# The second block's projections and its last product in three rounded passes each, with x kept in memory in between

## The reference, cut to what matters

```python
h = rms_norm_2(x, norm_g) * (1 + scale[:, None, :]) + shift[:, None, :]
proj = h @ w_in
q, kcr, vcr, ksl, vsl, kwn, vwn, z_a, g_br, u, z_s = jnp.split(proj, offs, axis=-1)
...
attn = nsa_attention(q, kc, vc, k_slc, kv_heads(vsl), k_win, kv_heads(vwn), gates)
attn = attn * jax.nn.silu(z_a)
y = s5_mixer(u, ssm_a_re, ssm_a_im, ssm_log_dt, ssm_b_re, ssm_b_im, ssm_c_re, ssm_c_im, ssm_d)
y = jax.nn.gelu(y)
y = y * jax.nn.sigmoid(y @ glu_w.astype(jnp.float32) + glu_b.astype(jnp.float32))
ssm = y.astype(x.dtype) * jax.nn.silu(z_s)
mix = jnp.concatenate([attn, ssm], axis=-1) @ w_out
return x + gate[:, None, :] * mix
```

## Time and profile before

| | us |
|---|---|
| median of 3 runs | 1591.18 (1590.16 to 1595.38) |
| the profiled execution | 1588.68 |
| its span (first to last instruction) | 1586.8 |
| TensorE busy | 1432.6 (90%) |
| VectorE busy | 950.3 (60%) |
| ScalarE busy | 511.9 (32%) |
| GpSimd busy | 52.7 (3%) |
| second block from its first product to the GLU | 1144.4 to 1348.4 |
| attention pairs | 1397.7 to 1528.2 |
| last product, from its first halves to its last matmul | 1519.35 to 1579.1 |

### The profile page before, as it was taken

The page is one execution under the profiler, slowest core; times in us unless marked ns, Lnnn a source line. Parts: engine busy times, 40 slices in busy tenths (PEclk is TensorE's granted clock), DMA queues, the critical chain, the costliest instruction groups (busy, mean ns, idle before and its releaser), DMA issues.

```text
span 1586.8 us, 18674 instructions
## 1 busy us (share of the span) xinstructions
PE 1432.6 (90%) x7046; PEld 1092.9 (69%) x7046; DVE 950.3 (60%) x1601; ACT 511.9 (32%) x824; POOL 52.7 (3%) x43
## 2 busy tenths in 40 slices
PE   5998888896989877999899999999798999988998
PEld 4758788785567655787688888888567954566653
DVE  6259767676166768774545545533493748868730
ACT  5346332331322554233323423423313221223310
POOL 0000000000000450000000000000000002000000
PEclk9999999997989979999899999999898999989999
DMA  5212111121222120353134443222421122520001
GB/s 223 75 53 81 67 41 54 61 90 49 84 107 80 47 74 27 136 209 107 53 136 156 186 159 143 73 77 106 133 82 37 58 76 80 186 80 1 1 1 53
DMA packets 39881, 140.49 MB, mean 89 GB/s; under 512 B 13041, under 2 KB 17521, under 8 KB 27249
## 3 DMA queue, kind: packets, MB, share of 16 engines
q1 hardware_dynamic: 34608, 130.53, 23.4%
q10 hardware_dynamic: 5184, 8.78, 1.5%
HBM read 128.42 MB, written 8.39 MB: 86 GB/s over the span
## 4 chain that ended last, share of the span: by engine, by line
PE 54%; DVE 4%; ACT 1%; issue 1%; ACTq 0%; DVEq 0%
PE turn L700 22%; PE score L685 7%; PE score L700 5%; PE sum L685 4%; PE turn L685 3%; PE sum L700 2%; PE sum L1263 2%; PE sum L1145 1%; PE score L1145 1%; PE score L1237 1%; PE turn L1249 1%; PE turn L822 1%; DVE stat L2541 1%; PE turn L1118 1%; DVE probs L1774 0%
## 5 line engine op out<-in xcount | busy, mean ns | idle before, releaser
L1816 DVE TENSOR_TENSOR ring_r<-ring,heads_r 128x1024 fp32r<-128x1024 f32 (+3 forms) x153 | 176.3, 1153 | 222.6 <-ACT heads_r L1359 187.2
L1359 ACT ACTIVATE heads_r<-ring 128x1024 fp32r<-128x1024 f32 (+3 forms) x153 | 153.4, 1002 | 241.0 <-DMA ring<-wstream 129.2
L700 PE MATMUL score<-h_sb_r,heads_r 128*128 128x512 f32 x376 | 151.6, 403 | 0.0
L700 PE MATMUL turn<-tiles_r,heads_r 128*128 128x512 f32 x336 | 132.2, 393 | 0.0
L700 PE MATMUL turn<-h_sb_r,heads_r 128*128 128x512 f32 x304 | 119.7, 394 | 8.1 <-DVE ring_r L1816 8.1
L700 PE MATMUL turn<-wide_r,heads_r 128*128 128x512 f32 x312 | 121.9, 391 | 0.0
L700 PE MATMUL turn<-wide_r,ring_r 128*128 128x512 f32 x312 | 121.6, 390 | 0.0
L700 PE MATMUL score<-x_sb_r,heads_r 128*128 128x512 f32 x256 | 110.1, 430 | 8.9 <-DVE ring_r L1816 6.5
L700 PE MATMUL score<-x_sb_r,ring_r 128*128 128x512 f32 x256 | 103.8, 405 | 0.0
L700 PEld LDWEIGHTS score<-h_sb_r,heads_r 128*128 128x128 f32 x376 | 73.9, 197 | 13.9 <-issue 0.2
L700 PEld LDWEIGHTS turn<-tiles_r,heads_r 128*128 128x128 f32 x336 | 64.1, 191 | 13.3
(11 more groups left out here) (399 smaller groups left out, 2952.5 us busy)
## 6 DMA issues: line engine op xcount, KB each, us to landing
ring<-wstream SPq DMA_DIRECT2D x95, 1024.0 KB, 4.9
ring<-wstream SPq DMA_DIRECT2D x16, 704.0 KB, 4.4
ring<-gated SPq DMA_DIRECT2D x6, 1024.0 KB, 6.9
gated<-tiles ACTq DMA_DIRECT2D x15, 256.0 KB, 2.0
gated<-probs ACTq DMA_DIRECT2D x9, 256.0 KB, 2.0
x_sb<-xT SPq DMA_DIRECT2D x4, 512.0 KB, 5.7
x_sb<-xT ACTq DMA_DIRECT2D x1, 2048.0 KB, 8.3
outT<-x_sb SPq DMA_DIRECT2D x1, 2048.0 KB, 6.3
```

The costliest lines, as they stand in the source:

```text
L700: return pe.matmul(out, a, w, **k) if moving else pe.matmul(out, w, a, **k)
L1359: step(act.activation(head_piece(p), chunk(name)[:, c:c + cols], ACT.Identity), f"head {p}")
L1816: step(dve.tensor_tensor(out, a, b, op), name)
```

## The change

- The chunks of `w_in` and `w_out` of the second block get pieces: 23 for `w_in` (22 of 1024 columns, one of 192), 8 for `w_out`. All products with them go through `triple`. In the first pair of products TensorE follows the splits k by k (`split_pair`).
- The rounded activations of the norm need two buffers. The head goes where x lies (`X_HEAD` in `x_sb`), the remainder into `h_sb`. So ScalarE stores each of the eight tiles of x to memory (`gated`) as soon as it is complete and loads all back (2 MB) behind the last product of `w_in`.
- The heads of the 23 pieces get six places of their own (`PLACES2`: an unused constant, the mask `chosen`, four pairs of tiles), since `heads` holds state-space data there. `heads_through` says how many ScalarE makes after each drain: one to four pieces ahead.
- The remainders of all 31 pieces, the scaling of x (16 operations instead of VectorE's 8), the splits of the four state-space tiles and of three attention tiles are GpSimd's. VectorE splits the norm (8 operations more) and the last attention tile.
- Order: 14 products instead of 9 after the first ones stand ahead of the matrices (2 whole, 12 row), so 3 row products more than before; `SIDE` is 5, 5, 4, 4, and 18 are left, so no product is left for behind the last y.
- `w_out`: four banks instead of two take first halves: two in the place of the 33rd pair, one ahead of the last turn, one behind it; then four second halves and four whole products.

```diff
-    proj2 = [(f"proj2_{i}", len(c) * tile) for i, c in enumerate(by_twos(PROJ2))]
-    out += proj2[:2] + [(f"rows2_{n}", KD * width(parts)) for n, parts in ROWS2] + proj2[2:]
+    proj2 = [(f"proj2_{i}", [tile] * len(c)) for i, c in enumerate(by_twos(PROJ2))]
+    out += proj2[:2] + [(f"rows2_{n}", [KD * 24] if n == "g" else [tile, tile]) for n, _ in ROWS2] + proj2[2:]
...
-    out += [(f"wout2_{i}", 2 * tile) for i in range(4)]
+    out += [(f"wout2_{i}", [tile] * 2) for i in range(4)]
...
-    SIDE = [5, 5, 5, 4]
+    SIDE = [5, 5, 4, 4]
...
+    WIDE_HEAD = H_REST
+    WIDE_REST = [TL_REST[:, 6 + k if k < 4 else k - 2, :] for k in range(KD)]
+    WIDE_BANKS = [score[:, z * T:(z + 1) * T] for z in range(4)]
...
+    FIRST2, WOUT2 = piece_of["proj2_0"][0][0], piece_of["wout2_0"][0][0]
+    PLACES2 = [cst_r[:, coff["level"][0]:coff["level"][0] + PIECE], chosen_r[:, :]] + \
+              [tiles_r[:, (6 + 2 * z) * T:(8 + 2 * z) * T] for z in range(4)]
+    HOME2 = [0, 1, 2, 3, 4, 5, 0, 1, 2, 3, 4, 5, 2, 0, 1, 4, 5, 4, 5, 0, 1, 0, 1]
...
+    def home_free(q):
+        earlier = [i for i in range(q) if HOME2[i] == HOME2[q]]
+        return earlier[-1] + 1 if earlier else 0
+    def heads_through(q):
+        n = q + 1
+        while n < len(HOME2) and n <= q + 4 and home_free(n) <= q + 1:
+            n += 1
+        return FIRST2 + n
     def head_piece(p):
+        if FIRST2 <= p < WOUT2:
+            return PLACES2[HOME2[p - FIRST2]][:, 0:pieces[p][2]]
         return heads_r[:, p % PIECES * PIECE:p % PIECES * PIECE + pieces[p][2]]
...
-                    pe.wait_ge(dve_step, at(f"split {p}"))
+                    pe.wait_ge(pool_step if p >= FIRST2 else dve_step, at(f"split {p}"))
...
-            first = feature_units("proj2", PROJ2, lambda k: H[:, k, :], ready=(act_step, [f"normed block2 {k}" for k in range(KD)]))
-            units = itertools.chain(*[row_units(f"rows2_{n}", width(parts), H) for n, parts in ROWS2], first)
-            run(first, 4)
-            run(units, 9)
+            acts2 = [(X_HEAD[:, k, :], H_REST[:, k, :]) for k in range(KD)]
+            outs = [gemm_bank()]
+            up(gemm_full)
+            outs.append(gemm_bank())
+            for mm in split_pair(outs, [("proj2_0", 0), ("proj2_0", KD * P)], acts2, [f"split block2 {k}" for k in range(KD)]):
+                mm.then_inc(gemm_full, 1)
+            up(gemm_full, "used proj2_0")
+            def whole_units(first, last):
+                for i in range(first, last):
+                    for e in range(2):
+                        split_product(gemm_bank()[:, :], f"proj2_{i}", e * KD * P, acts2).then_inc(gemm_full, 1)
+                        up(gemm_full, f"used proj2_{i}" if e else None)
+                        yield
+            units = itertools.chain(whole_units(1, 2), *[split_rows(f"rows2_{n}", width(parts), acts2) for n, parts in ROWS2], whole_units(2, 7))
+            run(units, 14)
...
+            def wide_half(e, first):
+                for k in range(4, KD) if first else range(4):
+                    if first and e == 0:
+                        pe.wait_ge(pool_step, at(f"split ssm {k - 4}"))
+                    mm = triple(WIDE_BANKS[e], f"wout2_{e // 2}", (e % 2 * KD + k) * P, P, WIDE_HEAD[:, k, :], WIDE_REST[k],
+                                k == 4, k == 3, k == 3)
+                if not first:
+                    mm.then_inc(score_full, 1)
...
-                    w = have("wout2_0").rearrange("p (c k n) -> p c k n", c=2, k=KD)
-                    for k in range(4, KD):
-                        for e in range(2):
-                            pe.matmul(S[e], w[:, e, k, :], TL[:, k - 2, :], start=(k == 4), stop=False)
+                    wide_half(0, True)
+                    wide_half(1, True)
+            pe.wait_ge(score_done, at("pair probs 63"))
+            wide_half(2, True)
             turn_attention(3)
-            pe.wait_ge(turn_done, at("attn T 3"))
-            for e in range(2):
-                for k in range(4):
-                    mm = pe.matmul(S[e], w[:, e, k, :], TL[:, 6 + k, :], start=False, stop=(k == 3))
-                mm.then_inc(score_full, 1)
+            wide_half(3, True)
+            for n in range(NT):
+                pe.wait_ge(dve_step if n == NT - 1 else pool_step, at(f"split late {n}"))
+            for e in range(4):
+                wide_half(e, False)
                 up(score_full, f"full wout2 {e}")
-            feature_tiles("wout2", range(8), lambda k: TL[:, 6 + k if k < 4 else k - 2, :], to_turn=True, first=1)
+            acts = [(WIDE_HEAD[:, k, :], WIDE_REST[k]) for k in range(KD)]
+            for j in range(4, 8):
+                split_product(turn_bank()[:, :], f"wout2_{j // 2}", j % 2 * KD * P, acts).then_inc(turn_full, 1)
+                up(turn_full)
...
+                    if FIRST2 <= p < WOUT2:
+                        if home_free(p - FIRST2):
+                            act.wait_ge(heads_used, FIRST2 + home_free(p - FIRST2))
+                    elif p >= PIECES:
                         act.wait_ge(heads_used, p - PIECES + 1)
...
+                else:
+                    weight_heads(2)
                 act.wait_ge(turn_done, at(f"added final {j}"))
+                act.dma_start(gated[j], X[:, j, :]).then_inc(parked, 16)
...
+            act.wait_ge(parked, 16 * KD)
             for k in range(KD):
                 act.wait_ge(dve_step, at(f"scaled block2 {k}"))
-                step(act.activation(H[:, k, :], H[:, k, :], ACT.Identity, bias=MOD[:, k:k + 1]), f"normed block2 {k}")
+                step(act.activation(X_HEAD[:, k, :], H[:, k, :], ACT.Identity, bias=MOD[:, k:k + 1]), f"head block2 {k}")
...
+                        k_ = PROJ2.index((n, i))
+                        weight_heads(upto=heads_through(piece_of[f"proj2_{k_ // 2}"][k_ % 2][0] - FIRST2))
...
-            for _ in range(13):
+            for _ in range(16):
...
+            act.dma_start(X, gated[0:KD].rearrange("b p t -> p b t")).then_inc(x_again, 16)
...
+                if i in (20, 22, 24, 26):
+                    j = (i - 20) // 2
+                    head(f"ssm {j}", WIDE_HEAD[:, 4 + j, :], TL[:, 2 + j, :])
+                if i in (42, 44, 46, 48):
+                    if i == 42:
+                        act.wait_ge(turn_done, at("cmp added 3"))
+                    weight_heads()
+                if i in (50, 58):
+                    attention_head((i - 50) // 8)
+            for n in range(2, NT):
+                attention_head(n)
+            weight_heads(4)
...
+            def rest_of_block2(k):
+                dve.wait_ge(act_step, at(f"head block2 {k}"))
+                stt(H_REST[:, k, :], H[:, k, :], MOD[:, k:k + 1], X_HEAD[:, k, :].bitcast(F32), ALU.add, ALU.subtract, f"split block2 {k}")
+            scale_by_spread("block2", lambda k: GAIN2[:, k:k + 1], H, "scaled", lambda k: k and rest_of_block2(k - 1))
+            rest_of_block2(KD - 1)
...
-            for k in range(KD):
-                stt(X[:, k, :], X[:, k, :], sm("g_final")[:, k:k + 1], rstd_final, ALU.mult, ALU.mult)
...
+            tile = TL[:, 6:10, 3 * P:]
+            split("attn T 3", tile, WIDE_HEAD[:, 0:4, 3 * P:], tiles_r[:, 6 * T:10 * T].rearrange("p (k t) -> p k t", k=4)[:, :, 3 * P:])
+            tally.named["split late 3"] = tally.named["split attn T 3"]
+            dve.wait_ge(pool_step, at("x scaled"))
+            for j in range(4):
                 dve.wait_ge(score_full, at(f"full wout2 {j}"))
-                stt(X[:, j, :], S[j], MOD[:, 16 + j:17 + j], X[:, j, :], ALU.mult, ALU.add)
-            add_to_x(lambda j: MOD[:, 16 + j:17 + j], first=2)
+                stt(X[:, j, :], WIDE_BANKS[j], MOD[:, 16 + j:17 + j], X[:, j, :], ALU.mult, ALU.add)
+            add_to_x(lambda j: MOD[:, 16 + j:17 + j], first=4)
...
+                    for p in range(FIRST2, WOUT2):
+                        of, c, cols = pieces[p]
+                        pool.wait_ge(act_step, at(f"head {p}"))
+                        step(pool.tensor_tensor(chunk(of, ring_r)[:, c:c + cols], chunk(of)[:, c:c + cols], head_piece(p).bitcast(F32), ALU.subtract),
+                             f"split {p}")
...
+            for j in range(4):
+                pool.wait_ge(act_step, at(f"head ssm {j}"))
+                step(pool.tensor_tensor(WIDE_REST[4 + j], TL[:, 2 + j, :], WIDE_HEAD[:, 4 + j, :].bitcast(F32), ALU.subtract), f"split ssm {j}")
+            pool.wait_ge(x_again, 16)
+            rstd_final = part(wide, 4816, T)
+            for k in range(KD):
+                step(pool.tensor_scalar(X[:, k, :], X[:, k, :], sm("g_final")[:, k:k + 1], None, ALU.mult))
+                step(pool.tensor_tensor(X[:, k, :], X[:, k, :], rstd_final, ALU.mult), "x scaled" if k == KD - 1 else None)
+            for p in range(WOUT2, WOUT2 + 4):
+                weight_rest(p)
+            for n in range(3):
+                pool.wait_ge(act_step, at(f"head attn T {n}"))
+                cols = slice(n * P, (n + 1) * P)
```

(5 more changed lines are left out.)

22 lines of the change are left out of this document (17 added, 5 removed).

## The result

The changed kernel takes **1602.14 us** (median of 4 runs, 1601.96 to 1604.75); the kernel before, run beside it, 1591.05 (1590.16 to 1595.38). The ratio is 1.0071, with a 95% interval of 1.0048 to 1.0094: slower, where the prediction said 18 us faster. Its profiled execution has a span of 1599.9 us against 1586.8.

What follows compares the result with a forecast made beforehand. TensorE's time per product was taken to bound the kernel from 1144 us on. Terms: -7.3 up to the attention, +2.5 in it, -13.4 in the last product, sum -18.2, giving 1573 us as median; range 1563 to 1589.

Steps and rivals of the forecast that it cites:

- 8, VectorE: Matrix building: matrices 6.3 us later within 8.2 of slack, so nothing; VectorE's chain behind the states +0.5.
- 1, parking x: Ahead of the norm's square: the last of eight stores of x on ScalarE costs +0.4 us.
- 2, first pair: First pair of products, second block: VectorE's alternating scalings and remainders set the pace; -1.9 us, between -2.1 and +0.3.
- 3, 4: Twelve whole products of w_in at 5.44 us, not 6.87: -17.2; sixteen row products at 2.88, not 3.455: -9.2.
- 5, the gate rows: Four gate-row products, 24 wide, at 2.64 us against 1.79 or 1.7: +3.6, bounds 0 and +4.
- 6, the transfers: Between last state-space product and GLU: the 16 transfers lose their cover; +15.0 us, bounds +11 and +17.
- 7, the pieces: Weight pieces through ScalarE and GpSimd: 2.8 to 3.5 us each on GpSimd, +1.5 us with all.
- 9, attention: Attention: ScalarE's heads between exponentials cost 0 to 8.0 us, taken as +2.5; GpSimd's scaling and splits run beside.
- 10, last product: From first halves to the last matmul: 46.4 us instead of 59.8, -13.4.
- GpSimd blocks VectorE: Rival, matrix building and diagonals: each GpSimd piece halts VectorE for its whole time; 1590 us, chance 0.17.
- GpSimd is the new bound: Rival, weight pieces: a remainder takes much longer, 7 us a piece; 1597 us, slower than before, chance 0.07.
- the bare transfers cost less: Rival, ahead of the GLU: 15 becomes 11, attention heads and pieces cost 0; 1565 us, chance 0.16.

Runs made afterwards that it cites:

- e4: The changed kernel with side counts 5, 5, 4, 2, leaving two whole products behind the last state-space product; 1602.95 us.
- e5: e1 with side counts 5, 5, 4, 2, so that two whole products cover the 16 transfers; 1584.21 us.
- e1: The changed kernel with the 23 projection weight remainders replaced by one-input GpSimd operations (zeros in their place); 1590.77 us.
- e7: e2 with every GpSimd operation of the attention having one input instead of two (those remainders are zeros); 1577.43 us.
- e2: The kernel before with the last product alone in three passes, heads on ScalarE, remainders on GpSimd; 1585.68 us.
- e6: The changed kernel with 21 of the 23 weight remainders made by VectorE and side counts 5, 5, 4, 2; 1582.91 us.
- e9: e6 with three memsets moved to GpSimd and VectorE's 'blocks k' ahead of the ropes of k; 1583.86 us.
- e8: The kernel before with additional GpSimd operations of five forms beside VectorE's two-input operations in the matrix building; 1588.15 us.
- e13: e2 with the remainders of the four state-space tiles and the first four last-product weight pieces made by VectorE; 1580.75 us.
- the filler: e11 with 14 unread products on TensorE's queue in its wait between the compress products; 1576.29 us.
- e11: e9 with x scaled by VectorE behind the last attention tile and the last product's first eight remainders on VectorE; 1580.42 us.
- e15: e11 run once more, unchanged; 1582.07 us.
- e16: e11 with 7 unread products, in place of 14, in TensorE's wait between the compress products; 1581.08 us.

## Why the prediction was wrong

The step that failed is 8, VectorE, together with the reading under it that GpSimd doesn't hold VectorE up. By its own steps, up to the first pair (forecast -7.3, measured +15.8, a miss of 23.1, of which the lock is 12.4):

- **1, parking x.** TensorE's sums ahead of the norm start at 1134.01 instead of 1132.82: +1.2, not +0.4.
- **2, first pair.** Scaling starts at 1146.41, 3.8 late, of which 2.6 are the two diagonals under GpSimd's third and fourth piece: a cost that stood only in the rival. From there the pair takes 15.2 us (its row products start at 1172.52, two products of 5.44 earlier is 1161.6), not 13.6. With the 0.8 of term 1 TensorE is through with its units at 1207.1 instead of 1202.1: 5.0 of the miss.
- **3, 4.** 5.44 and 2.88 us at full clock, as forecast; but the whole product behind the gate rows took 7.92, 2.5 more.
- **5, the gate rows.** 2.58 at full clock, as forecast; but two of the four ran at half clock, and all four together took 14.7 us for before's 8.2: +6.5 instead of +3.6, outside the bounds of 0 to 4. "That is so before and after" was wrong: before, only the third stood at half clock. In exchange the outputs y behind them, 4.8 us at half clock before, take 2.7 at full now (-2.1).
- **8, VectorE.** "8.2 us of slack, so nothing". Nine halts of 2.1 us made the building 19.1 longer; the matrices came at 1216.8, and TensorE waited 9.8.
- **6, the transfers.** 15.4 us of wait for 13: "I take nothing for it", of the 2 MB read back, is what was wrong, since the 16 landed in 6.2 us for 2.0 and do so only where that load is issued beside them. The half clock behind the wait cost the 2 us of the forecast (GLU to compress products 15.9 for 13.8). e4 and e5 say more: this wasn't a term of the sum, since with the cover back (e4) nothing is gained at the end; VectorE's chain, priced at +0.5, was as late.
- **7, the pieces.** 2.4 to 2.9 us each, and TensorE never waited for one of `w_in`: 0 instead of +1.5. "With two inputs not less" was wrong: two inputs take 2.40 undisturbed, one input (e1) 2.95. The Trainium skill (GPSIMD Engine Reference, "Elementwise — side-by-side cycle accounting"), whose 4497 ns for 2048 columns made an estimate of 2.25 us, was nearer than the range of 2.8 to 3.5.
- **9, attention.** +10.9 instead of +2.5. By the table: 4.4 in pairs 21 to 24, of which 2.9 go with the second input by e7; 0.8 in the last stretch; 2.3 in pairs 1 to 8, where the granted clock is 0.80, 0.50, 0.50 in the first 24 us for before's 1.00, 0.78, 0.58; and 3.4 in pairs 9 to 16, of which e2, with before's clock, has 0.8; the rest stands beside a granted clock of 0.60 and 0.79 in two of its 8 us windows (before 0.79 and 1.00).
- **10, last product.** 59.8 to 46.2: -13.6 for -13.4. Right.

From the first state-space product to the first pair the miss is 8.3. Its parts: 1.7 for the first small products, at half clock behind the wait of 9.8 (9.8 us for 8.1); 2.9 and 2.5 for the gate rows and the product behind them; -2.1 for y; 2.4 for the transfers; -1.5 for the pieces; 1.9 between the first compress product and the first pair (37.9 for 35.5, forecast +0.5). That is 7.8; the last 0.5 I can't place. So 5.0 + 9.8 + 8.3 = 23.1; and 15.8 + 10.9 - 13.6 = 13.1, which is the difference of the spans.

Two steps gave a wrong sign to the whole. The first is the reading of the earlier trace rows: GpSimd's 5.88 us operation beside VectorE's 0.69 us one was taken as evidence that VectorE isn't held, though I wrote myself that this operation hardly reads. An operation on 32 columns that computes for 5.88 us says nothing about one that reads 2 x 1024 columns. The rival *GpSimd blocks VectorE* had the mechanism, the place and nearly the count (eight pieces, nine halts; 14.4 us forecast, which by its own factors is 14.2; 9.8 + 2.6 found), and a chance of 0.17. Its total, 1590, is still 12 short: it kept the forecast for the gate rows, the transfers and the attention. The Trainium skill (SBUF — State Buffer, "Who interferes with whom") says that a VectorE instruction with two SBUF inputs contends with a GpSimd instruction that reads SBUF and not with one that only writes it, and calls the ports that the two share an exclusive lock. The traces agree for two inputs (2.7 for 0.69) and for memset (nothing); for one input they show less than a lock for the whole instruction (1.41).

The second is the independence of the terms. I added gains on TensorE's path and took each cover by itself. e1 is the changed kernel with most of the halts gone, and its pairs start where before's do, not 7.3 earlier; e5 and e6 cover the transfers, and theirs start 0.8 earlier and 1.5 later. In e4, e5 and e6 VectorE's chain from the states to the blocks and ropes was next; in e1 it was the bare transfers. Only with halts, cover and that chain mended together (e9) do the pairs start 5.9 earlier.

The rival *GpSimd is the new bound* is refuted by 2.4 to 2.9 us a piece, *the bare transfers cost less* by 15.4.

## What to carry to other kernels

Work that is handed to GpSimd is not free because GpSimd is idle: here a remainder of 2.4 to 2.9 us delays the VectorE operation with two SBUF inputs that starts beside it by 2.1 us, and VectorE makes that remainder itself in 1.23 (e6). What only writes (the memsets of e8 and e9) held nothing up, and GpSimd's scaling of x beside the attention, where many of VectorE's operations read PSUM, cost nothing that the table shows. A price read at full clock (the gate rows) holds only where the clock is full, so look at the granted clock of the rows around it before and ask what the change makes of them. When a forecast gives two engines' chains the same arrival within a few us, a gain on one of them is worth at most the gap to the other, so cost the second chain before adding terms; of this change the last product alone, with remainders on VectorE (e13), keeps as much as everything together without the filler (e11, e15).

## What the runs showed of the hardware that I had not expected

- GpSimd's one-input 1024-wide operation (2.9 to 3.0 us) delays VectorE's two-input one by 0.72 us and not to its end; a broadcast column as its second input makes it a two-input one (2.27).
- A one-input VectorE operation is held too. In the changed kernel, at a remainder of GpSimd:

```profile
1255.40 2.57 DVE L1904 TENSOR_SCALAR heads<-rows 128x512 f32<-128x512 f32 x1
```

  It takes 0.43 otherwise, at 1217.55. VectorE's operations with one input in PSUM keep their times beside GpSimd (424 ns in both kernels' attention for the 128x256 product of sums and reciprocals).
- A product in float32 leaves two matmul rows of 0.44 us for 512 columns, so 14 of them are 12.28 us: the filler was twice what I had written down. With it the pairs start 2.1 us later than in e15 and the clock recovers early; with half of it (e16) they start 1.7 earlier and it doesn't.
- 16 transfers of 64 KB land in 6.2 us as a median when a load of 2 MB on another queue is issued beside them, and in 2.0 when it comes behind them.
- Which length the low stretch of the granted clock behind the pairs' start takes can be worth 5.6 us (36.6 against 31.0 for eight pairs with the same instructions). What decides it is open.
